# Stores of the experts' results: issued by ScalarE on its own DMA queue instead of by SyncE between the loads of weights

## The reference, cut to what matters

```python
g_idx = argmax(x @ w_gr + b_gr)               # one of 4 groups
top_v, top_i = top_k(e_logits of that group, 2)   # two of its 8 experts
def expert_block(tok_b, e):                   # for each of 32 experts
    h = silu(xb @ w_gate[e]) * (xb @ w_up[e]) # 1024 -> 512
    return h @ w_down[e]                      # 512 -> 1024
y[token] += weight * out                      # each token has two results
```

## Time and profile before

| | us |
|---|---|
| median of 3 runs | 1660.17 |
| lowest, highest | 1656.58, 1660.31 |
| the profiled execution | 1661.11 |
| its span, first to last instruction | 1659.4 |
| TensorE busy in the span | 1412.8 (85%) |
| VectorE, ScalarE busy | 682.1, 479.2 |
| loads of weights, SP's queue | 132 of 2048 KB each |
| stores of first and second blocks | 46 of 128 KB each |

### The profile page before, as it was taken

How to read it: one execution, slowest core, us unless ns; L and a number is a source line. 1 busy time by engine, 2 the same in 40 slices (tenths; PEclk the granted TensorE clock), 3 DMA queues, 4 the chain that set the end, 5 groups by cost and what they waited for, 6 DMA issues and landing times.

```text
span 1659.4 us, 24134 instructions
## 1 busy us (share of the span) xinstructions
PE 1412.8 (85%) x9624; PEld 1060.5 (64%) x9624; DVE 682.1 (41%) x1238; ACT 479.2 (29%) x753; POOL 40.2 (2%) x79
## 2 busy tenths in 40 slices
PE   6999997878866767796544999997999999999976
PEld 5786776645544443364223888875888888888865
DVE  4576745110111001010006656445436666656645
ACT  5452431000000000000015222233334444444432
POOL 2000000000000000000011100000000000000000
PEclk9998997989988899999876999997999999999988
DMA  8937324898999973399956555210221212121101
GB/s 351 398 127 279 127 102 203 326 406 361 380 379 423 383 327 152 139 410 395 422 224 247 214 203 182 109 52 27 102 102 51 102 52 102 52 102 52 51 1 64
DMA packets 38375, 339.26 MB, mean 204 GB/s; under 512 B 3784, under 2 KB 9800, under 8 KB 19400
## 3 DMA queue, kind: packets, MB, share of 16 engines
q1 hardware_dynamic: 30584, 302.33, 45.7%
q0 software_dynamic: 7200, 34.08, 5.8%
q10 hardware_dynamic: 432, 0.60, 0.1%
HBM read 312.62 MB, written 24.38 MB: 203 GB/s over the span
## 4 chain that ended last, share of the span: by engine, by line
PE 42%; DMA 4%; DVE 3%; ACT 2%; SPq 1%; issue 1%; POOL 0%; DVEq 0%; ACTq 0%; PEldq 0%; POOLq 0%
PE ps L285 41%; DMA y_scratch<-ar 4%; PE ps L732 1%; SPq L2087 1%; ACT ar L882 0%; DVE b_NL L1326 0%; DMA ar<-y_scratch,rt 0%; DVE ar L1318 0%; DVE hres L1796 0%; DVE hres L1789 0%; ACT b_NH L891 0%; DVE ar L1979 0%; ACT ar L1110 0%; ACT ar L1106 0%; DVE ar L1277 0%
## 5 line engine op out<-in xcount | busy, mean ns | idle before, releaser
L285 PE MATMUL ps<-ar 128*32 128x256 f32 (+5 forms) x1486 | 267.4, 397 | 53.7 <-ACT ar L1026 20.8
L285 PEld LDWEIGHTS ps<-ar 128*128 128x128 f32 (+3 forms) x1486 | 178.2, 163 | 128.5 <-issue 91.4
L285 PE MATMUL ps<-ring,ar 128*32 128x256 f32 (+1 forms) x2272 | 200.8, 411 | 47.6 <-DMA ring<-in_wts_dram 15.1
L285 PE MATMUL ps<-b_NH,b_WH 128*128 128x512 f32 x704 | 187.1, 401 | 9.5 <-ACT b_NH L891 5.1
L285 PE MATMUL ps<-b_NH,b_WL 128*128 128x512 f32 x704 | 181.0, 393 | 0.0
L1259 DVE TENSOR_TENSOR b_WL<-ring,b_WH 128x1024 fp32r<-128x1024 f32 x112 | 136.5, 1220 | 99.7 <-ACT b_WH L834 99.7
L285 PEld LDWEIGHTS ps<-ring,ar 128*32 128x32 f32 (+1 forms) x2272 | 105.4, 117 | 109.8 <-issue 61.3
L285 PE MATMUL ps<-b_NL,b_WH 128*128 128x512 f32 x704 | 173.7, 389 | 0.0
L285 PE MATMUL ps<-spare,ar 128*32 128x256 f32 (+1 forms) x1680 | 138.6, 415 | 39.4 <-ACT ar L1023 13.2
L834 ACT ACTIVATE b_WH<-ring 128x1024 fp32r<-128x1024 f32 x112 | 118.1, 1055 | 162.8 <-PE ps L285 159.8
L1689 DVE TENSOR_TENSOR ar<-ar,ps 128x128 f32<-128x128 f32 x46 | 13.1, 287 | 361.9 <-ACT ar L1020 358.6
(11 more groups left out here) (267 smaller groups left out, 1655.5 us busy)
## 6 DMA issues: line engine op xcount, KB each, us to landing
ring<-in_wts_dram SPq DMA_DIRECT2D x84, 2048.0 KB, 16.2
spare<-in_wts_dram SPq DMA_DIRECT2D x36, 2048.0 KB, 21.1
ar<-in_wts_dram SPq DMA_DIRECT2D x12, 2048.0 KB, 18.7
y_scratch<-gate POOLq DMA_DIRECT2D x15, 1024.0 KB, 25.5
ring<-in_wmod_dram SPq DMA_DIRECT2D x24, 512.0 KB, 4.6
ar<-in_wmod_dram POOLq DMA_DIRECT2D x24, 512.0 KB, 4.3
y_scratch<-ar SPq DMA_DIRECT2D x50, 128.0 KB, 2.3
hres<-in_x_dram SPq DMA_DIRECT2D x4, 512.0 KB, 6.8
```

What stands on the lines that cost most here:

```text
L285: return pe.matmul(o, l, m, start=start, stop=stop, skip_group_check=True)
```

## The change

All stores of experts' results leave SP. ScalarE issues them on its own queue, each right behind the copy that fills its tile, after a wait for that copy's own semaphore. The `Else` branches that waited for `oy` and `ty` and raised them are ScalarE's too. SP's loop keeps only the loads; before those of an expert with a third block it waits for TensorE's last matmul of that block (`t_d2`) instead of for its copy. The same is done for overflow blocks, of which these inputs have none. Tiles, semaphores, shapes of transfers and the order of all else stay.

```diff
 ScalarE, expert n:
                 if n >= 2:
                     act.wait_ge(S[f"y{s}"], 16 * (n // 2))
                 copy_y(s, 5).then_inc(S["m_y"], 1)
+                act.wait_ge(S["m_y"], n + 1)
+                store(n, s).then_inc(S[f"y{s}"], 16)
                 with act.If(second(n)):
...
                     if n:
                         act.wait_ge(S["oy"], 16 * n)
                     copy_y(2, 7).then_inc(S["o_y"], 1)
+                    act.wait_ge(S["o_y"], n + 1)
+                    store(NE + n, 2).then_inc(S["oy"], 16)
                 with act.Else():
                     if n:
                         act.wait_ge(S["o_ht"], n)
                         act.wait_ge(S["o_y"], n)
+                        act.wait_ge(S["oy"], 16 * n)
                     act.sem_inc(S["o_ht"], 1)
                     act.sem_inc(S["o_y"], 1)
+                    act.sem_inc(S["oy"], 16)
...
 third_block(u):
                 act.activation(ysb3, ps[:, 7, :], ACT.Copy).then_inc(S["t_y"], 1)
+                act.wait_ge(S["t_y"], u + 1)
+                store_third(u)
 SyncE:
             for n in range(NE):
                 with sp.If(third(n)):
-                    sp.wait_ge(S["t_y"], n + 1)
-                    if n:
-                        sp.wait_ge(S["ty"], 32 * n)
-                    store_third(n)
-                with sp.Else():
-                    if n:
-                        sp.wait_ge(S["ty"], 32 * n)
-                    sp.sem_inc(S["ty"], 32)
+                    sp.wait_ge(S["t_d2"], n + 1)
                 for m in range(3):
                     i = P_MOE + 3 * n + m + 8
                     if i < P_C0:
                         load(i)
...
-                sp.wait_ge(S["m_y"], n + 1)
-                store(n, n % 2).then_inc(S[f"y{n % 2}"], 16)
-                with sp.If(second(n)):
-                    sp.wait_ge(S["o_y"], n + 1)
-                    if n:
-                        sp.wait_ge(S["oy"], 16 * n)
-                    store(NE + n, 2).then_inc(S["oy"], 16)
-                with sp.Else():
-                    if n:
-                        sp.wait_ge(S["oy"], 16 * n)
-                    sp.sem_inc(S["oy"], 16)
```

More of the change, by code:

```diff
@@ L1026, in copy_y, with store, store_third @@
                 return act.activation(ysb[s], ps[:, b, 0:256], ACT.Copy)
+            def store(n, s):
+                return act.dma_start(y_d[n * CAP:(n + 1) * CAP, :].rearrange("t (q c) -> q t c", q=4), ysb[s])
+            def store_third(u):
+                r = 2 * NE * CAP + WIDE * u
+                for hf in range(2):
+                    act.dma_start(y_d[r:r + WIDE, hf * 512:(hf + 1) * 512],
+                                 ysb3[64 * hf:64 * hf + 64, :]).then_inc(S["ty"], 16)
             def third_block(u):
@@ L1088, in scalar_program @@
                             act.wait_ge(S[v], n)
+                        act.wait_ge(S["ty"], 32 * n)
                     for v in ("t_xg", "t_sg", "t_ht", "t_y"):
                         act.sem_inc(S[v], 1)
+                    act.sem_inc(S["ty"], 32)
             for j in range(NOV):
@@ L2169, in sync_program @@
                     expert(0, 2).then_inc(S["v_w0"], 16)
-                    sp.wait_ge(S["t_y"], NE + j + 1)
-                    sp.wait_ge(S["ty"], 32 * (NE + j))
-                    store_third(NE + j)
+                    sp.wait_ge(S["t_d2"], NE + j + 1)
                     sp.wait_ge(S["ty"], 32 * (NE + j + 1))
```

## The result

The changed kernel takes 1692.91 us (median of 4 runs, 1690.71 to 1693.13); the kernel before took 1659.93 beside it (4 runs, 1656.58 to 1660.31). The ratio is 1.020, 95% interval 1.018 to 1.022: slower by 33 us. The profiled execution took 1693.13 us, span 1691.4, and by its own time lies 32 above that of before.

What follows compares the result with a forecast made beforehand. Weights and PE were taken to bound the kernel in turns. Costs of +56 us less 19 at third blocks gave +37 on the profiled 1661.11, 1698, given as 1697 for the median; 8-in-10 range 1652 to 1735.

Steps and rivals of the forecast that it cites:

- One packet for one: On DMA engines sharing two queues: packets alternate one for one whatever their size, so each store packet lets a weight packet pass.
- Rival B: On ACT's queue: a store passes as a block and lands in 4 to 6 us; 1640 us in all, chance 0.14.
- Landings of 21 and 42 us: On ACT's queue beside weights: 21.1 us for one store to land, 42 for the second of a pair.
- the walk: Expert by expert through the stage, how much later copies come than before; costs sum to +56 us before the third blocks' gain.
- ACT's waits about 200 us, DMA share 0.79, stage end near 900: Expert stage: ACT's store waits grow from 132.6 us, DMA share falls from 0.84, and the end moves from 862.
- The stands at `oy`: ACT, in experts without a second block: new waits of 12 to 24 us in experts 2, 10, 17 and 24.
- Third blocks -19: At third blocks weights have run out, stores land in about 4 us; PE's 14.25 and 6.58 us become 0.75: -19.
- The second way: Check by the four engines' idle time: nine dry spells of 7 us plus 28 at third blocks, 91 against 55, +36.
- Costs at nothing: Small terms: SP's earlier loads 0, at most 4 us; issuing on ACT 2 us; PE's 30.6 us of sequencer stands stay.
- C: Expert stage: new waits fall where PE waits for weights anyway; +20 is paid by third blocks' 19; 1660 us, chance 0.09.
- D: Expert stage: each pair of stores costs a full dry spell, fourteen of 8 us; 1746 us, chance 0.07.
- E: Third blocks: loads still wait for matmuls, landings stay as before, ACT's 8 us of issues remain; 1669 us, chance 0.05.

## Why the prediction was right, step by step

The forecast was 1697, the result 1692.91; the sum was +37, the profiled executions differ by 32.

- **One packet for one.** Right, and shown by 32 against 31 per engine in 18 us, by 17.6 against 17.3, by the store's packets coming in fours every 0.65 us, and by halved packets that halve the waits. The counts of the earlier trace rows, on which I had rested it, did not decide it alone: blocks of equal length would give them too. Rival B, the block pass, would have given 1640 and landings of 4 to 6 us; it is out. The Trainium skill (DMA: Bandwidth & Descriptors, "Queues, rings and completion order") has an engine drain a whole packet of some 9 to 17 descriptors before it turns to another ring; at the packets that this trace records no such block is seen (four on four engines, then none for 0.35 us, then four), and the measurement decides.
- **Landings of 21 and 42 us.** Measured 23.6 for a store with an empty queue before it and, where weights kept flowing for most of the time, 37 and 40 for the second of a pair. Many stores fit neither: single ones close behind each other took 32.5 to 38.9, the growing backlog that the walk had only as +5, and where weights had run out 3.73 sufficed, as for the last.
- **ACT's waits about 200 us, DMA share 0.79, stage end near 900.** 198.3, 0.80 and 894.8 (the last store, issued at 891.06, lands after 3.73). PE's 14.25 below 1: 0.70.
- **The stands at `oy`.** Predicted in experts 2, 10, 17 and 24 with 12 to 24 us; they were in 2, 8, 17 and 24, with 14.8 to 26.9.
- **The walk.** Its sum was closer than its terms. Expert 3: predicted +15, was +18.2. From there to expert 5 the kernel won back 5.7, which the walk didn't have. Experts 6 to 11 together +23: was +18.8 (12.5 to 31.3), but the three pairs were paid at expert 8's `Else` in one stand of 26.9 us, and expert 10, for which I had given +10 and an `oy` wait, had none and won 5 back: a long dry spell leaves nothing for the next. Experts 12 to 18 +5: was +4 (31.3 to 35.7 at expert 19). Third blocks -19: was -21.6 (35.7 to 14.1), of which PE's two stands, 20.8 to 1.4 us, are 19.4. Experts 22 and 23 +15: was +19. From there to the end -2: was -1.
- **The second way.** It gave the four engines 510 us of work and 91 idle; the stage has 597 us, so 87 idle. But it counted nine dry spells of 7 us. Taken 2 us at a time, the DMA share falls under 0.3 in five places outside the third blocks and the tail (near 355, 469, 591, 619 and 763 us), some of them longer than 7. That sum agrees in part by luck.
- **Costs at nothing.** The earlier `t_d2`: I took 0, at most 4; alone it is worth about 3. Issues on ACT: 2 us; no run separates them. PE's own stands stay: 30.6 to 32.4.
- **The other rivals.** C (1660) had dry spells at two or three places; there were five, and the time lies outside it. D (1746) had fourteen, one for each pair. E (1669): the third blocks' gain is there, and landings did not stay.
- **What the prediction didn't see.** I wrote that in SP's queue 1.6 us is all that a store adds. Spreading them over sixteen engines is worth 30 to 33 us in the old kernel, so that kernel was not at its bound either. And I took the change as one thing: it is a gain of 19 (second and third blocks) and a cost of 52 (first blocks).

## What to carry to other kernels

Before a small store is moved from behind the big loads to a queue of its own, count its packets on the busiest DMA engine, add those of stores still under way, and multiply by what one packet of the neighbour takes: that is about its landing, and whatever waits for it must have that much slack. Then look at the outer dimension of the transfer: a store on four engines has four times as many packets on each as one on sixteen. Spreading it was worth 2% in SP's queue and 4% in ACT's. Where a change moves several kinds of stores, run each kind alone.

## What the runs showed of the hardware that I had not expected

- A DMA's two contiguous halves, written as two, were joined: 24192 packets on q1 in the whole execution, with the view and without it; as two DMAs of half the columns there are 43200.
- The same 128 KB in four DMAs instead of one, on an engine that has other things to do, cost little: 2.73 us for the four issues of the last store on ScalarE, where nothing hides them, and still the shortest time.
- 46 stores of 1.6 us on four of sixteen DMA engines, 74 us of their time, went with 30 to 33 us of the kernel before (stores' landings and loads not told apart), and the DMA share of its stage rose from 0.84 to 0.88 once they were spread.
- One issue of SP's lasted 15.2 us as a single instruction; there were 37 of over 2 us in the stage of the kernel before, and none in that of the changed kernel, whose SP issues loads only.
